# Forgetting attention as one stream of tiles, with the next pair's projections and the memory attention set between the tiles

## The reference, cut to what matters

```
h = rmsnorm(x, g)                                  # (2048, 1024) of one sequence
q, k, v, f, mq = split(h @ w_in_fox)               # 12 heads of 64 | ... | 12 logits | 4 heads of 64
c = cumsum(log_sigmoid(f + b_forget))              # one column per head
s[t, u] = q_t . k_u / 8 + c[t] - c[u]              # causal: u <= t only
self_out = softmax(s) @ v                          # 12 heads
mem_out  = softmax(mq @ mk^T / 8) @ mv             # 4 heads, 256 memory tokens
mixed = concat(self_out, mem_out)                  # (2048, 1024), then @ w_out
```

## Time and profile before

| what | value |
|---|---|
| median of 3 runs | 4574.43 us (4568.94 to 4780.07) |
| the profiled execution | 4576.19 us |
| its span, slowest core | 4574.4 us (all cores 4553.5 to 4574.4) |
| TensorE busy, share of the span | 3654.3 us, 80% |
| ScalarE | 1858.9 us, 41% |
| VectorE | 1625.8 us, 36% |
| GpSimd | 766.5 us, 17% |
| mean granted TensorE clock | 0.903 (0.900 to 0.907 over the cores) |
| layer 1 from the first `mq` matmul to `out_proj`, sequence 0 | 1102.67 to 1673.0 us |
| the same, sequence 1 | 3379.86 to 3948.6 us |

### The profile page before, as it was taken

One profiled execution on the slowest core, in us unless ns is written; L12 is line 12 of the kernel. 1 busy time (PEld: TensorE's weight loads), 2 busy tenths in 40 slices (PEclk: granted clock), 3 DMA queues, 4 the chain that ended last, 5 costly groups with the idle time before them and its releaser, 6 DMA issues.

```text
span 4574.4 us, 60097 instructions; the slowest of 8 cores (4553.5 to 4574.4 us)
## 1 busy us (share of the span) xinstructions
PE 3654.3 (80%) x18816; PEld 1655.1 (36%) x19144; DVE 1625.8 (36%) x2915; ACT 1858.9 (41%) x3237; POOL 766.5 (17%) x1034
## 2 busy tenths in 40 slices
PE   2598699996687886999836986999966878869997
PEld 1253244442333332443313532444413333324443
DVE  3564531413332225222236645214133323252322
ACT  2477331314557653222025663313155575632220
POOL 0263121211000002111112621112110000021211
PEclk9698899996899997999967977999968999979998
DMA  4142154542000012446432411545410000125554
GB/s 123 37 89 43 19 75 67 74 67 37 10 13 10 8 19 31 73 69 141 76 98 44 87 37 22 76 66 75 67 30 10 15 8 13 17 35 72 86 90 85
DMA packets 133295, 241.64 MB, mean 53 GB/s; under 512 B 15232, under 2 KB 19328, under 8 KB 132992
## 3 DMA queue, kind: packets, MB, share of 16 engines
q0 software_dynamic: 94176, 171.48, 26.1%
q1 hardware_dynamic: 38816, 66.29, 5.1%
HBM read 367.12 MB, written 16.78 MB: 84 GB/s over the span
## 4 chain that ended last, share of the span: by engine, by line
PE 68%; DVE 8%; issue 7%; ACT 7%; DMA 5%; POOL 2%; SPq 1%; another core or an unknown queue 1%; DVEq 0%; ACTq 0%; POOLq 0%
PE pb L886 19%; PE pb L876 18%; PE pb L678 13%; PE pb L862 5%; PE pb L851 3%; ACT scrB L1032 2%; PE pb L703 2%; POOL xT_s L1409 2%; DMA wr_s<-wall 2%; DVE scrF L1196 2%; DMA mixT_s<-scrF 1%; ACT rl_s L987 1%; PE pb L767 1%; PE pb L759 1%; DVE hT_s L1184 1%
## 5 line engine op out<-in xcount | busy, mean ns | idle before, releaser
L876 PE MATMUL pb<-hT_s,wr_s 128*128 128x512 bf16 x4012 | 903.3, 384 | 41.0 <-DMA wr_s<-wall 27.0
L1394 POOL DMA_DIRECT2D wr_s<-wall x636 | 339.7, 534 | 3062.3 <-PE pb L678 1190.2
L1032 ACT ACTIVATE scrB<-pb,small_s 128x512 bf16<-128x512 f32 x960 | 521.9, 636 | 313.7 <-PE pb L854 292.0
L876 PEld LDWEIGHTS pb<-hT_s,wr_s 128*128 128x128 bf16 x4096 | 403.8, 99 | 538.4 <-issue 72.2
L1133 ACT ACTIVATE scrB<-pb 128x512 bf16<-128x512 f32 x512 | 305.7, 597 | 628.7 <-PE pb L876 617.1
L886 PE MATMUL pb<-mixT_s,wr_s 128*128 128x512 bf16 x2006 | 470.1, 385 | 2.6 <-ACT scrF L968 0.2
L862 PE MATMUL pb<-scrB,u2hi_s 128*128 128x512 bf16 (+3 forms) x936 | 335.9, 359 | 154.3 <-ACT scrB L1032 147.8
L886 PE MATMUL pb<-u2hi_s,wr_s 128*128 128x512 bf16 x2006 | 451.6, 379 | 2.0
L678 PE MATMUL pb<-hT_s,wr_s 128*128 128x512 bf16 x1670 | 409.5, 392 | 25.7 <-DVE hT_s L1184 16.5
L703 PE MATMUL pb<-scrF,cbf_s 128*128 128x512 bf16 x252 | 115.6, 513 | 359.7 <-ACT scrF L968 358.4
L1379 DVE CAST hT_s<-pb 128x512 bf16<-128x512 f32 x128 | 82.5, 686 | 835.9 <-PE pb L886 810.5
(11 more groups left out here) (141 smaller groups left out, 4017.2 us busy)
## 6 DMA issues: line engine op xcount, KB each, us to landing
wr_s<-wall POOLq DMA_DIRECT2D x636, 256.0 KB, 3.9
mixT_s<-scrF SPq DMA_DIRECT2D x192, 128.0 KB, 2.4
xT_s<-xT SPq DMA_DIRECT2D x8, 2048.0 KB, 18.9
outT<-xT_s SPq DMA_DIRECT2D x8, 2048.0 KB, 9.4
u2hi_s<-wall POOLq DMA_DIRECT2D x18, 256.0 KB, 5.9
u2hi_s<-memT SPq DMA_DIRECT2D x32, 128.0 KB, 7.2
rl_s<-pos SPq DMA_DIRECT2D x8, 256.0 KB, 3.6
xT_s<-cin SPq DMA_DIRECT2D x1, 576.0 KB, 7.0
```

The costliest lines, as they stand in the source:

```text
L876: ins = pe.matmul(pb[:], lhsT=wu[:, k, :], rhs=hT[:, k, bsl(b)], start=k == 0, stop=k == 7)
L1032: act.activation(out=pt[:, 0:wd], in_=at("fs", s, p, i)[:, 0:wd], func=AF.Exp, bias=dcol[:, kt, 2 * p + hh:2 * p + hh + 1], scale=0.125).t ...
L1394: pool.dma_start(out=buf[slot], in_=wall_d[wall_idx[unit]]).then_inc(*M.at(f"w_{slot}", n, 16))
```

## The change

Memory attention of layer 1 is no longer a stage of its own, and the 6 pairs of heads are one stream of 480 + 32 tiles (`fox_stream`). The 480 are ordered by pair, block of queries, head, tile of keys (before: head, then block). Between the tiles stand pieces of projection, called `fill`: half a block's q, k or `mq` (4 matmuls of 512 columns) or half a block's v (16 matmuls of 128 columns). They are spread evenly over the tiles of a block of queries:

- in block 0 of pair p: q of block 1 (2 pieces beside 8 tiles);
- in block 1: q of block 2 and k block 0 of pair p+1 (4 pieces, 16 tiles);
- in block 2: q of block 3 and k blocks 1 to 3 of pair p+1 (8 pieces, 24 tiles);
- in block 3: v of pair p+1 and its q block 0 (10 pieces, 32 tiles);
- in blocks 2 and 3 of pairs 0 to 3 also `mq` of one block (2 pieces) and its 4 tiles of memory attention.

Keys and values have two buffers each (`KX`, `VX`), q is held by block in `R0` and `R1`, `mq` by block in `F0` and `F1`. The casts of q and k are the same as before. Those of v take 4 tiles at once. The row `drow` is copied into each q block by two DMAs (48 per sequence; before 12). The memsets are GpSimd's. All projections use banks 6 and 7. Weights of the stream have four slots (`W4`), `mq` one of its own (`MW`). Ahead of the stream stand k, v and the first q block of pair 0, together with `fl`, `fsum` and `frow`.

```
+def fox_stream():
+    stream, tiles = [], []
+    for p in range(6):
+        for qb in range(NBLK):
+            here = [("f", p, qb, hh, kt) for hh in range(2) for kt in range(4 * qb + 4)]
+            fills = [("q", p, qb + 1)] if qb < 3 else []
+            if p < 5:
+                if qb == 1:
+                    fills += [("k", p + 1, 0)]
+                elif qb == 2:
+                    fills += [("k", p + 1, b) for b in range(1, 4)]
+                elif qb == 3:
+                    fills += [("v", p + 1, b) for b in range(4)] + [("q", p + 1, 0)]
+            if p < 4 and qb >= 2:
+                u, mb = p // 2, 2 * (p % 2) + qb - 2
+                fills = [("mq", u, mb)] + fills
+                here += [("m", u, mb, hh, kt) for hh in range(2) for kt in range(2)]
+            pieces = [f + (part,) for f in fills for part in range(2)]
+            done = 0
+            for i, tile in enumerate(here):
+                stream.append(("tile", len(tiles)))
+                tiles.append(tile)
+                while done < len(pieces) and (2 * done + 1) * len(here) <= 2 * (i + 1) * len(pieces):
+                    stream.append(("fill",) + pieces[done])
+                    done += 1
+            stream += [("fill",) + f for f in pieces[done:]]
+    return stream, tiles
...
@@ make_plan, fox @@
+        for b in range(NBLK):
+            for part in range(2):
+                fill("k", 0, b, part)
         P.take(AB, ("tb", s), ("carry", (s, NT - 2)))
         P.take(AB, ("db", s), ("dcol", s))
         P.add("fsum", s)
+        for b in range(NBLK):
+            for part in range(2):
+                fill("v", 0, b, part)
         for g in range(NBLK):
             P.take(P4, ("rb", s, g), ("drow", (s, g)))
             P.add("frow", s, g)
...
+        for part in range(2):
+            fill("q", 0, 0, part)
...
@@ make_plan, layer 1 @@
                 norm(s, l, 0, range(NBLK))
-                mem_attn(s, l)
+                P.open(("X2", "X3"), ("fox", s), ("memh", (s, l, 7)))
                 fox(s, l)
...
@@ pe_program @@
+            def fill(s, t, p, b, part):
...
+                for k in range(4 * part, 4 * part + 4):
+                    w.wait_ge("nout", (s, 1, 0, b, k))
+                    ins = pe.matmul(bank[:], lhsT=wu[:, k, :], rhs=hT[:, k, bsl(b)], start=k == 0, stop=k == 7)
+                if part == 1:
+                    ins.then_inc(*M.at(key[0], key[1:]))
...
@@ pool_program @@
+                elif kind == "fset":
+                    s, = k
+                    w.wait_ge("memh", (s, 1, 7))
+                    for i in range(2):
+                        pool.memset(buf[f"VX{i}"][:, :, 64:128], 1.0).then_inc(*M.at("fset", (s, "v", f"VX{i}")))
+                    w.wait_ge("mv", (s, 1, 1, 1))
+                    w.wait_ge("fset", (s, "v", "VX1"))
+                    for i in range(2):
+                        pool.memset(buf[f"KX{i}"][64:128, :, :], 0.0).then_inc(*M.at("fset", (s, "k0", i)))
+                        w.wait_ge("fset", (s, "k0", i))
+                        pool.memset(buf[f"KX{i}"][64:65, :, :], 1.0).then_inc(*M.at("fset", (s, "k1", i)))
+                        w.wait_ge("fset", (s, "k1", i))
+                elif kind == "fqz":
+                    z = pspot("fqz", *k)
+                    pool.memset(z[64:128, :], 0.0).then_inc(*M.at("fqz", tuple(k)))
+                    w.wait_ge("fqz", tuple(k))
...
@@ sp_program @@
+                elif kind == "fill" and k[1] == "q" and k[4] == 1:
...
+                    w.wait_ge("drow", (s, b))
+                    for hh in range(2):
+                        sp.dma_start(out=qx(("qx", s, p, b))[64:65, hh, :], in_=tab[2 * p + hh:2 * p + hh + 1, bsl(b)]).then_inc(
```

More of the change, by code:

```diff
@@ L399, in fox, with fill @@
     def fox(s, l):
+        stream, tiles = fox_stream()
+        last = {}
+        for i, tile in enumerate(tiles):
+            last[tile[:2]] = i
+            last[tile[:3]] = i
+            last[tile[:4]] = i
         P.add("fset", s)
+        for i in range(2):
+            P.take(RS, ("fqz", s, i), ("fqz", (s, i)))
+            P.add("fqz", s, i)
         P.take(AB, ("fl", s), ("fadd", s))
         P.add("fl", s)
-        P.weight(W3, ("f", l, 0), s, ("fl", s))
+        P.weight(W4, ("f", l, 0), s, ("fl", s))
+        def fill(t, p, b, part):
+            if part == 0:
+                if t == "v":
+                    P.take(SM, ("fv", s, p, b), ("fve", (s, p, b)))
+                    if b == 0:
+                        P.take(VX, ("vx", s, p), ("fpv", (s, last[("f", p)])))
+                elif t == "mq":
+                    P.take(SM, ("mq", s, l, p, b), ("mqc", (s, l, p, b)))
+                    P.take(MQ, ("mqt", s, p, b), ("fs", (s, last[("m", p, b)])))
+                else:
+                    P.take(SM, ("f" + t, s, p, b), ("fe" + t, (s, p, b, 1)))
+                    if t == "q":
+                        P.take(RS, ("qx", s, p, b), ("fs", (s, last[("f", p, b)])))
+                    elif b == 0:
+                        P.take(KX, ("kx", s, p), ("fs", (s, last[("f", p)])))
+            P.add("fill", s, t, p, b, part)
+            if part == 1 and b == 3:
+                if t == "mq":
+                    P.weight(MW, ("mq", l, p), s, ("mq", (s, l, p, b)))
+                else:
+                    P.weight(W4, (t, l, p), s, ("f" + t, (s, p, b)))
+        for b in range(NBLK):
+            for part in range(2):
+                fill("k", 0, b, part)
         P.take(AB, ("tb", s), ("carry", (s, NT - 2)))
@@ L409, in fox @@
             P.add("frow", s, g)
[L410 to L431, removed]
+        for part in range(2):
+            fill("q", 0, 0, part)
+        n = len(tiles)
+        for kind, *k in stream:
+            if kind == "fill":
+                fill(*k)
+                continue
+            i, = k
+            m, p, qb, hh, kt = tiles[i]
+            chunk = p if m == "f" else 6 + p
+            if kt == 0:
+                P.take(OB, ("fo", s, m, p, qb, hh), ("mix", (s, l, chunk, hh, qb)))
+                P.take(RL, ("rl", s, l, chunk, hh, qb), ("mix", (s, l, chunk, hh, qb)))
+            P.take(P4, ("fs", s, i), ("fex", (s, i)))
+            P.take(BS, ("fp", s, i), ("fpv", (s, i)))
+            P.add("ft", s, i)
+        for i in range(n, n + AHEAD):
+            P.add("ft", s, i)
     def out_proj(s, l):
@@ L761, in pv @@
                 ins.then_inc(*M.at("pv", (s, h, b)))
[L763 to L768, removed]
             def rs(s, h, b):
@@ new lines, in fill @@
+            def fill(s, t, p, b, part):
+                if t == "v":
+                    bank = spot("fv", s, p, b) if part == 0 else at("fv", s, p, b)
+                    wu = weights(("v", 1, p), s)
+                    for i in range(2 * part, 2 * part + 2):
+                        for k in range(NCH):
+                            w.wait_ge("nout", (s, 1, 0, b, k))
+                            ins = pe.matmul(bank[:, tsl(i)], lhsT=hT[:, k, tsl(4 * b + i)], rhs=wu[:, k, :],
+                                            start=k == 0, stop=k == 7)
+                    if part == 1:
+                        ins.then_inc(*M.at("fv", (s, p, b)))
+                    return
+                key = ("mq", s, 1, p, b) if t == "mq" else ("f" + t, s, p, b)
+                bank = spot(*key) if part == 0 else at(*key)
+                wu = weights((t, 1, p), s)
+                for k in range(4 * part, 4 * part + 4):
+                    w.wait_ge("nout", (s, 1, 0, b, k))
+                    ins = pe.matmul(bank[:], lhsT=wu[:, k, :], rhs=hT[:, k, bsl(b)], start=k == 0, stop=k == 7)
+                if part == 1:
+                    ins.then_inc(*M.at(key[0], key[1:]))
@@ L1113, in act_program @@
                         *M.at("drow", (s, g)))
-                elif kind == "fa":
-                    fa(*k)
+                elif kind == "ft":
+                    ft(*k)
+                elif kind == "fill":
+                    s, t, p, b, part = k
+                    if t == "mq" and part == 1:
+                        out = spot("mqt", s, p, b)
+                        half = out[:].bitcast(BF)[:, 0:BLK]
+                        w.wait_ge("mq", (s, 1, p, b))
+                        act.activation(out=half, in_=at("mq", s, 1, p, b)[:], func=AF.Copy).then_inc(*M.at("mqc", (s, 1, p, b)))
                 elif kind == "op":
```

200 lines of the change are left out of this document (106 added, 94 removed).

## The result

The changed kernel takes 4431.99 us (median) against 4573.43 before: ratio 0.969, 95% interval 0.967 to 0.971. The change is faster by 142 us. The forecast was 4310, 266 us faster, and its range ended at 4400: the direction is right, but little more than half of the forecast gain is there.

The account below looks back on a forecast made before the run. ScalarE was taken as the fuller engine in the stream. Start 35.7 plus six pairs 400.9 made a stretch of 436.6 us, saving 265.8 from 4576.19 over two sequences: 4310 us, range 4240 to 4400.

Parts of the forecast that it names:

- What bounds the kernel: Layer 1, norm to output projection: TensorE and ScalarE take turns; after the change ScalarE stays fuller, by 3.6 us in pairs 0 to 3.
- the work of a pair: In the stream: TensorE 52.6 us, ScalarE 52.2; with memory attention in pairs 0 to 3, 59.6 and 63.2.
- What a piece costs: Projection piece between attention tiles: a 1.58 us chain against 1.16 of exponentials stops ScalarE by 0 to 0.42; half, 0.21, taken.
- Edits at nothing: Copies of `drow`, weight loads, casts of q, k and v, and the reorder by block: no cost counted.
- Rival 2: Projections stay serial because their two banks are emptied by VectorE behind multiplications waiting for `attn_end`: 4537 us, chance 0.06.
- Ahead of the stream: Work before the first scores, from 1102.67 to 1138.3: 35.7 us, in place of 110.33.
- Memsets: Moved to GpSimd, ahead of the stream: at the cheap bound, VectorE's rate of 0.85 ns an element, 16.5 us, adding 0.
- Rival 1: In the stream every piece is paid in full, and the dear memsets too: 4400 us, chance 0.12.
- the dear memsets: GpSimd memsets at its two-input rate, 2.49 ns an element, 48.4 us, delaying the first scores by some 16 us.
- Rival 3: TensorE at the lower of its two clock levels, the whole stream at 1.2 GHz: 4871 us, chance 0.05.
- Rival 4: Clock falls to 0.81 where TensorE is dense, making it the stream's bound: 4417 us, chance 0.03.

Follow-up runs that it names:

- both edits: Changed kernel with three tiles ahead instead of two and the two late q projections moved forward; 4312.2 to 4320.4 us, ratio 0.943 to the kernel before.
- e8_before3: Kernel before the change, with three tiles ahead instead of two in its forgetting attention; 4543.3 us against a median of 4579 for the kernel before.
- e10_quarter_a3q: Changed kernel with pieces of half the size, late q projections moved forward and three tiles ahead; 4307.5 and 4331.2 us, ratio 0.943 to the kernel before.
- early q: Changed kernel, next pair's q block 0 first in block 3, q block 1's pieces after tiles 0 and 1 in block 0; 4390.5 and 4395.7 us.

## Why the prediction was wrong, point by point

**What bounds the kernel: right; the work of a pair: nearly.** ScalarE's busy time in the stream is 362 to 366 us with whole pieces, against 357 by the sum. The sum took pair 0 for all six, and the middle ones are longer: in the kernel before, pairs 1 to 4 of sequence 0 keep ScalarE busy for 53.2 to 53.7 us of 56.7 to 57.7, where the sum has 52.2 of 54.5. With both edits the stream takes 400.6 us, where the forecast for the changed kernel was 400.9. That this is so close is partly luck: ScalarE works 361.6 us there and idles for 39.0, short gaps included, where the forecast had 357.2 and 43.7, 29.9 of them for stops at pieces, and score matmuls (L941) end only 2.4 us of its waits.

**What a piece costs: the step that failed.** The prediction wrote the chain down and made it 1.58 us, with hand-overs of 0.05; the trace has 1.78, with 0.14 from exponential to value matmul and 0.15 from scores to exponential. The 0.15 could be read before: in the earlier trace rows the scores end at 1334.27 + 0.63 = 1334.90 and the exponential starts at 1335.05. So the stop was bounded by 0.42 us and is 0.63 in block 3. Then it was halved, by no row, because some pieces would fall into a reciprocal's time. In the block of the rows above, three stops in a row are 0.64, 0.63 and 0.68. Paid in full, 0.63 for 142 pieces is 89 us a sequence; 29.9 stood in the sum. The measured price lies between: leaving out three quarters of the pieces' work took 54.5 us off the stream, 0.38 a piece, where 0.21 was counted, so this term was short by some 24.6 us a sequence. Three tiles of lead gave back 46.9 us, of which some 18 (half of the 36 of `e8_before3`) are not the pieces'. No run takes the pieces out altogether, so their full price stays open.

**Edits at nothing: the cast of q.** It was put at nothing, VectorE being less than half full. What was missed is not its load but its order. The sum counted 1.75 us of projection and two casts for the first q block only; of the later ones, q of block 1 and that of the next pair's block 0 stand at most two tiles before the scores that need them, and their casts behind a multiplication that waits for ScalarE. Rival 2 named this queue, for the banks, where the trace shows nothing of the kind, and overlooked q. The price: 21.1 us a sequence with two tiles of lead, 12.7 with three.

The two terms, 24.6 and 21.1, make 45.7 of the 59.2 us; how the rest divides, no run tells.

**Ahead of the stream:** 38.7 against 35.7. The 32 matmuls of k took 9.33 us at a granted clock of 0.76, where the sum had 7.0. v waited 2.71 us for its casts behind `fsum`'s chain on VectorE, which the sum had put beside TensorE's work; the matmuls of the gates came out shorter than the 10.2 us taken over. Memsets: right, at the bound taken.

```profile
1113.61:1122.94 9.33, 9.33 (x40) 3.85 (x37) 4.49 (x7) 0.82 (x2) 0.94 (x2) 0.76 0.19 30
```

**Rivals.** Rival 1 (every piece paid in full, 4400) was the nearest in time and in mechanism, though with the dear memsets, which didn't come. At the measured 0.63 a piece instead of 0.42 and without the memsets its stretch is 35.7 + 371.0 + 89.5 = 496, against 498.8 measured. That nearness is partly luck: it leaves q's casts out, and would have ScalarE work 357 us in the stream and idle for 13.8 + 89.5 = 103, where it works 366 and idles for 94. Rival 3 (low clock) did not come: 0.96 in the stream, though short lapses follow most of the waits for a cast. Rival 4 neither: at its densest, 354.88 of 400.60 us, the stream has 1.00. The Trainium skill ("TensorE: Matmul & The Clock Gate", Part 1, its note on the peak-current limiter) says that three cores of a die on dense matmuls bring 13/16 of full clock. In the profiled executions of the kernel before, of the changed kernel and of the one with both edits, none of the 8 cores was granted anything but 1.00 and 0.50. In `e10_quarter_a3q` the level of 0.81 did come, on the cores of one die and outside the stream. So as a rule for every dense stretch it differs from the measurement, and the measurement decides; but such a level exists on this chip, and no run here shows what brings it.

**Where the gain is.** By stretch, a sequence: memory attention 53.3 to 48.6 us; memsets, gates and the first projections 57.0 to 38.7; the pairs from the first scores on 460.0 to 411.5 (with memory attention apart). The three make 71.5. Of the 129 us in which TensorE projected alone in five pairs, 48.5 are hidden.

## What to carry to other kernels

In this kernel, work set between dependent steps held the other engine up until the lead covered the whole chain: the hand-over, the last step, the piece, the next step and the hand-over back. Write that chain with hand-overs from the trace, and if it is longer than what the other engine has queued, lengthen the lead or shorten the piece. Here, with early q, a third tile took 38.5 us off the stream and half-size pieces 17.3; both together took 41.9. Then follow what each piece makes through the queue of the engine that copies it out, by position and not by load. Three tiles ahead with the early q take 4318 us (median) against 4432; a fourth tile (4312) or half-size pieces (4307 and 4331) can't be told from it.

## What the runs showed that I had not expected

Where one engine had waited for the other, the value matmul started 0.14 us after the exponential's end, and the exponential 0.15 us after the scores' end (medians in the trace of the changed kernel). GpSimd sets 4096 bf16 elements a partition in 3.51 us, as fast as VectorE (3.47 us). TensorE's granted clock rose as its waits went: 0.96 in the stream of the changed kernel, 0.99 with either edit, 1.00 with both; it was 0.93 where the pieces' work was left out and 34.1 us of waits for casts stayed. And in one profiled execution the cores of one die were granted 0.81 for up to 185 us.
